# Block attention on Trainium2: two branches of one head group summed in one PSUM bank, the local one's probabilities scaled by GpSimd

## The reference, cut to what matters

```python
o_cmp = einsum(softmax(q @ kcmp - slope*dist), vcmp)          # p_c also picks the 8 blocks of o_sel
o_sel = einsum(softmax(q @ k_selected - slope*dist), v_selected)
o_win = einsum(softmax(q @ k_window - slope*dist), v_window)
gate  = sigmoid(gate_logits + gate_b)                         # three per head
o     = gate[..., 0:1]*o_cmp + gate[..., 1:2]*o_sel + gate[..., 2:3]*o_win
```

## Time and profile before

| | |
|---|---|
| runs | 4212.6, 4210.89, 4206.26 us; median 4210.89 |
| profiled execution | 4219.19 us |
| its span, first to last instruction | 4217.2 us |
| attention loop, first to last PE instruction | about 1591.7 to 2540.1 us |
| mean granted TensorE clock | 0.952 of 2.4 GHz |

### The profile page before, as it was taken

The page is one execution under the profiler, slowest core; times in us unless marked ns, Lnnn a source line. Parts: engine busy times, 40 slices in busy tenths (PEclk is TensorE's granted clock), DMA queues, the critical chain, the costliest instruction groups (busy, mean ns, idle before and its releaser), DMA issues. The chain is left out here.

```text
span 4217.2 us, 69303 instructions
## 1 busy us (share of the span) xinstructions
PE 3839.8 (91%) x26480; PEld 3139.9 (74%) x26481; DVE 2457.9 (58%) x4173; ACT 1996.7 (47%) x3165; POOL 578.8 (14%) x945
## 2 busy tenths in 40 slices
PE   7999999999988878999888877999599999999798
PEld 5777877777767646777777766999478888888687
DVE  2545555555556427777777655444576555567565
ACT  2434433344333216666666653222276555567565
POOL 1111111111121112112212210000110000001120
PEclk9999999999999978999999988999699999999899
DMA  4534434443333350000000006433388666689642
GB/s 129 152 99 111 134 107 111 123 118 92 106 98 88 78 123 23 14 13 19 16 19 19 21 13 190 133 124 105 150 332 325 235 237 228 226 318 363 252 149 94
DMA packets 512853, 557.18 MB, mean 132 GB/s; under 512 B 106188, under 2 KB 374476, under 8 KB 511532
## 3 DMA queue, kind: packets, MB, share of 16 engines
q1 hardware_dynamic: 479988, 461.10, 34.7%
q0 software_dynamic: 16416, 59.78, 3.8%
q10 hardware_dynamic: 16176, 32.55, 2.1%
HBM read 439.78 MB, written 113.57 MB: 131 GB/s over the span
## 5 line engine op out<-in xcount | busy, mean ns | idle before, releaser
L555 PE MATMUL fr_fb<-fr_hT_h,fr_w_h 128*128 128x512 f32 (+1 forms) x1312 | 536.1, 409 | 11.0 <-ACT fr_zs L836 7.6
L555 PE MATMUL fr_fb<-fr_hT_r,fr_w_h 128*128 128x512 f32 (+1 forms) x1312 | 531.9, 405 | 0.0
L555 PE MATMUL fr_fb<-fr_hT_h,fr_w_r 128*128 128x512 f32 (+1 forms) x1312 | 531.6, 405 | 0.0
L1005 DVE TENSOR_TENSOR fr_w_r<-fr_w_raw,fr_w_h 128x1024 fp32r<-128x1024 f32 (+1 forms) x164 | 197.9, 1207 | 498.4 <-ACT fr_w_h L809 497.4
L2065 DVE TENSOR_TENSOR aq_p_lo<-aq_t_bank,aq_p_hi 128x512 fp32r<-128x512 f32 x412 | 283.0, 689 | 192.1 <-ACT aq_p_hi L1958 184.8
L1958 ACT CAST aq_p_hi<-aq_t_bank 128x512 fp32r<-128x512 f32 x412 | 238.5, 581 | 249.7 <-PE aq_t_bank L1865 244.0
L836 ACT COPY fr_zs<-fr_fb 128x512 f32<-128x512 f32 (+1 forms) x148 | 87.0, 588 | 509.2 <-PE fr_fb L555 508.7
L555 PEld LDWEIGHTS fr_fb<-fr_hT_h,fr_w_h 128*128 128x128 f32 (+1 forms) x1312 | 248.8, 190 | 79.1 <-ACT fr_zs L836 13.2
L555 PEld LDWEIGHTS fr_fb<-fr_hT_h,fr_w_r 128*128 128x128 f32 (+1 forms) x1312 | 249.0, 190 | 63.4 <-issue 11.1
L555 PEld LDWEIGHTS fr_fb<-fr_hT_r,fr_w_h 128*128 128x128 f32 (+1 forms) x1312 | 249.1, 190 | 62.2 <-issue 10.9
L134 PE MATMUL ex_gu<-wx_gate_w,ex_xT 128*128 128x512 f32 x1176 | 288.5, 401 | 3.6 <-DVE ex_xT L2848 3.6
(11 more groups left out here) (495 smaller groups left out, 8672.0 us busy)
## 6 DMA issues: line engine op xcount, KB each, us to landing
wk_raw<-in_w_exp_gate_up SPq DMA_DIRECT2D x64, 2048.0 KB, 10.9
fr_w_raw<-in_w_in SPq DMA_DIRECT2D x160, 512.0 KB, 3.9
wk_raw<-in_w_exp_down SPq DMA_DIRECT2D x32, 2048.0 KB, 10.1
s_z<-fr_zs SPq DMA_DIRECT2D x160, 256.0 KB
s_rows<-ex_y ACTq DMA_DIRECT2D x50, 512.0 KB, 4.3
mx_mg<-s_z SPq DMA_DIRECT2D x32, 512.0 KB, 7.3
fr_zc<-s_z SPq DMA_DIRECT2D x15, 903.0 KB, 6.8
sh_shared<-in_x SPq DMA_DIRECT2D x16, 512.0 KB, 5.2
```

The source lines that it names most:

```text
L555: ins = pe.matmul(bank[0:cols_, :], (w_h, w_h, w_r)[p][:, k, c, 0:cols_].bitcast(F32R), (hT_h, hT_r, hT_h)[p][:, c, :].bitcast(F32R), star ...
L1005: dve.tensor_tensor(w_r[:, m % 2, :, 0:cols_].bitcast(F32R), w_raw[:, m % 2, :, 0:cols_], w_h[:, m % 2, :, 0:cols_], ALU.subtract).then_in ...
```

## The change

The units' order becomes selected, local, selected, local, both of the same pair. The pair's two units now share one sum in `o_bank`: the first `weigh` of the selected unit starts it and the last one of the local unit ends it. For that the local probabilities must carry the factor by which the local branch's weight differs from the selected one's. In the stage before, DVE turns gate 2 into gate 2 over gate 1, once. In the loop the new `ratios` (DVE, three small operations) makes that times the selected total over the local total, per head, and the new `scale` (POOL, four operations of up to 128x640) multiplies the local exponentials in place. A local unit's first `turn` waits for `scaled`. `ratios` and `scale` stand in step min(last run + 2, first turn - 1).

"back" comes once a pair, as four plain 128x128 transposes that fill `misc`; `combine` adds the halves by a reduction, multiplies by the weight and adds to y (three operations of 256 results each instead of four small ones or one). `take_out` comes once a pair, and waits for y instead of "back". "turn_y" moves behind the local unit of g = 1, that is two steps into the next selected unit. `select` always writes y by one DVE operation. "take_q" follows the last run of the local unit. `pair` goes. From t = 4 on the `small` places in `sc_even` and `sc_odd` begin with the selected unit.

```diff
         pairs = [(t, g) for t in reversed(range(NT)) for g in range(KV_HEADS)]
-        ahead = 2
-        self.units = [(t, g, WIN) for t, g in pairs[:ahead]]
-        for n, (t, g) in enumerate(pairs):
-            if n + ahead < len(pairs):
-                self.units.append((*pairs[n + ahead], WIN))
-            self.units.append((t, g, SEL))
+        self.units = [(t, g, b) for t, g in pairs for b in (SEL, WIN)]
         self.at = {unit: u for u, unit in enumerate(self.units)}
...
         f = self.first
-        self.small = self.at[WINDOW // P + 1, KV_HEADS - 1, SEL] + 1
+        self.small = self.at[WINDOW // P + 1, KV_HEADS - 1, WIN] + 1
         self.runs_at, self.run_end, self.begin, self.last = {}, [], [], []
...
             self.out_step[n] = later
-        self.out_step[0] = max(self.out_step[0], 6)
-        self.pe, self.act, self.dve, self.pool = {}, {}, {}, []
+        self.pe, self.act, self.dve, self.pool, self.ratios = {}, {}, {}, [], {}
         put = lambda table, step, *what: table.setdefault(step, []).append(what)
...
             if g == 0 and t + 2 < NT:
-                pool.append((self.last[self.at[t + 2, 1, SEL]] + 1, 2, n, "take_q", t, 0))
+                pool.append((self.last[self.at[t + 2, 1, WIN]] + 1, 2, n, "take_q", t, 0))
+            u = self.at[t, g, WIN]
+            step = min(self.last[u] + 2, f[u] - 1)
+            put(self.ratios, step, t, g)
+            pool.append((step, 1.5, n, "scale", t, g))
         self.lead = -min(m[0] for m in marks)
-        for u, (t, g, b) in enumerate(self.units):
-            marks.append((f[u + 1] + 2, 3, u, "back", t, 2 * g + b))
+        for n, (t, g) in enumerate(pairs):
+            marks.append((f[self.at[t, g, WIN] + 1] + 2, 3, n, "back", t, g))
         for t in range(NT):
-            marks.append((f[self.at[t, 1, SEL] + 1] + 3, 4, NT - t, "turn_y", t, 0))
+            marks.append((f[self.at[t, 1, WIN] + 1] + 3, 4, NT - t, "turn_y", t, 0))
         self.pool = [what[3:] for what in sorted(pool)]
...
             return ((0, 0), (1, 2 * (WINDOW + P)), (1, WINDOW + P), (1, 0))[(u - self.small) % 4]
-        return u % 2, RUN * (u // 2 % 2) if b == SEL and t < RUN // P else 0
+        return 1 if b == SEL else 0, RUN * (u // 2 % 2) if b == SEL and t < RUN // P else 0
...
     def reused(self, u):
-        return 5 <= u < len(self.units) and self.units[u][2] == self.units[u - 2][2] == SEL and self.units[u][0] >= RUN // P
+        return 2 <= u < len(self.units) and self.units[u][2] == SEL and self.units[u][0] >= RUN // P
...
         if u > self.at[RUN // P, KV_HEADS - 1, SEL]:
-            return (f[u - 1], (2 * f[u] + f[u - 1]) // 3) if u % 2 == 0 else (self.last[u - 1] + 1, f[u] - 2)
+            return (f[u - 1], (2 * f[u] + f[u - 1]) // 3) if self.units[u][2] == WIN else (self.last[u - 1] + 1, f[u] - 2)
         return f[u - 1], f[u] - 2
-
-    def out_is_first(self, t, g):
-        return self.misc["out", t, g] < self.misc["back", t, 2 * g + WIN]
...
-                step(pool.memset(pair[:, :], 0.0))
-                for d in range(2):
-                    masked(pair[:, :], [[-1, HD]], -d * HD, 1, 1.0, ALU.not_equal)
...
                 low(3)
+                by_branch = gates[:, :, :].rearrange("p t (h b) -> p b t h", b=3)
+                dve.wait_ge(g_done, 1)
+                dve.tensor_scalar(by_branch[:, 1, :, :], by_branch[:, 1, :, :], LEAST_GATE, None, ALU.max).then_inc(g_split, 1)
+                dve.wait_ge(g_split, 1)
+                dve.reciprocal(g_inv[:, :, :], by_branch[:, 1, :, :]).then_inc(g_split, 1)
+                dve.wait_ge(g_split, 2)
+                dve.tensor_tensor(by_branch[:, 2, :, :], by_branch[:, 2, :, :], g_inv[:, :, :], ALU.mult).then_inc(g_split, 1)
+                dve.wait_ge(g_split, 3)
                 dve.wait_ge(out_ok, 3)
...
                 def take_q(t):
-                    pool.wait_ge(s_made, F.run_end[F.at[t + 2, G - 1, SEL]])
+                    pool.wait_ge(s_made, F.run_end[F.at[t + 2, G - 1, WIN]])
                     split_q(pool, order(t))
...
                         pool.tensor_tensor(total_p, total_p, pct[0:N_CMP, h, :], ALU.add).then_inc(added, 1)
+
+                def scale(t, g):
+                    f, sc = front_no(t, g), sc_of(F.at[t, g, WIN])
+                    pool.wait_ge(ratio_ok, f + 1)
+                    for h in range(R):
+                        ins = pool.tensor_scalar(sc[:, h, :], sc[:, h, :], ratio[:, h:h + 1], None, ALU.mult)
+                    ins.then_inc(scaled, 1)
...
                     if kind == "back":
-                        pe.wait_ge(ot_ok, F.at[t, k // 2, k % 2] + 1)
+                        pe.wait_ge(ot_ok, front_no(t, k) + 1)
                         misc_free(n)
                         for h in range(R):
-                            ins = pe.matmul(misc[:, h * HD:(h + 1) * HD], oT[:, h, :], pair[:, :], start=True, stop=True)
+                            ins = pe.transpose(misc[:, h * P:(h + 1) * P], oT[:, h, :], ident[:, :])
                     if kind == "turn_y":
-                        pe.wait_ge(y_ok, F.at[t, G - 1, SEL] + 1)
+                        pe.wait_ge(y_ok, front_no(t, G - 1) + 1)
                         misc_free(n)
...
                     if n == F.first[u]:
-                        pe.wait_ge(exp_ok, R * (u + 1))
+                        t, g, b = F.units[u]
+                        if b == WIN:
+                            pe.wait_ge(scaled, front_no(t, g) + 1)
+                        else:
+                            pe.wait_ge(exp_ok, R * (u + 1))
                     if n >= 2:
...
                     t, g, b = F.units[u]
-                    first, last = n == F.first[u], n + 1 == F.first[u + 1]
+                    first, last = b == SEL and n == F.first[u], b == WIN and n + 1 == F.first[u + 1]
                     pe.wait_ge(lo_ok, n + 1)
                     if first and u:
-                        pe.wait_ge(ot_ok, u)
+                        pe.wait_ge(ot_ok, front_no(t, g))
                     for p in (p_hi, p_lo):
...
                         act.copy(flat(pct[0:N_CMP, :, :]), misc[0:N_CMP, :]).then_inc(misc_read, 1)
-                    if kind == "out" and F.out_is_first(t, k):
-                        act.wait_ge(misc_made, n + 1)
-                        act.wait_ge(imp_ok, f + 1)
-                        for h in range(R):
-                            c = 3 * (k * R + h)
-                            ins = act.activation(y[:, t % Y, k, h, :], misc[:, h * HD:(h + 1) * HD], ACT.Copy, scale=gates[:, t, c:c + 1])
-                        ins.then_inc(misc_read, 1)
                     if kind == "turn_y":
...
                 def take_out(n, u):
+                    t, g, b = F.units[u]
                     act.wait_ge(pv_made, n - 1)
-                    if u:
-                        t, g, b = F.units[u - 1]
-                        act.wait_ge(misc_made, F.misc["back", t, 2 * g + b] + 1)
+                    if u > 1:
+                        act.wait_ge(y_ok, front_no(t, g))
                     act.copy(flat(oT[:, :, :]), o_bank[:, :]).then_inc(ot_ok, 1)
...
                     ended = F.block[n - 2][0] if 0 <= n - 2 < F.n and n - 1 == F.first[F.block[n - 2][0] + 1] else None
+                    if ended is not None and F.units[ended][2] == SEL:
+                        ended = None
                     early = ended is not None and n > F.first[ended] + 2
...
                 v = Chain(dve, vec)
+                gate_of = lambda t, g, b: gates[:, t, 3 * R * g:3 * R * (g + 1)].rearrange("p (h b) -> p b h", b=3)[:, b, :]
+                wide_heads = lambda a: a.rearrange("p (h o) -> p h o", o=1).to_broadcast([P, R, HD])
...
-                def add_scaled(t, g, scale_of):
-                    for h in range(R):
-                        ins = dve.scalar_tensor_tensor(out=y[:, t % Y, g, h, :], in0=misc[:, h * HD:(h + 1) * HD], scalar=scale_of(h),
-                                                       in1=y[:, t % Y, g, h, :], op0=ALU.mult, op1=ALU.add)
-                    return ins
-
                 def select(n, t, g):
...
                     dve.wait_ge(misc_made, n + 1)
+                    if f:
+                        dve.wait_ge(sel_ok, f)
                     dve.tensor_tensor(imp[:, :], misc[:, R * HD:R * HD + N_SEL], keep_t[:, at], ALU.mult).then_inc(imp_ok, 1)
                     dve.wait_ge(imp_ok, f + 1)
-                    if not F.out_is_first(t, g):
-                        v.link(add_scaled(t, g, lambda h: gates[:, t, 3 * (g * R + h):3 * (g * R + h) + 1]))
-                        dve.sem_inc(misc_read, 1)
+                    v.link(dve.tensor_tensor(y[:, t % Y, g, :, :], misc[:, 0:R * HD].rearrange("p (h d) -> p h d", h=R),
+                                             wide_heads(gate_of(t, g, 0)), ALU.mult))
+                    dve.sem_inc(misc_read, 1)
                     v.link(dve.tensor_tensor(imp[:, :], imp[:, :], force_t[:, at], ALU.add))
...
```

(33 more changed lines are left out.)

16 lines of the change are left out of this document (10 added, 6 removed).

## The result

The change makes the kernel slower: 4325.4 us (4321.8 to 4328.6, four runs) against 4209.4 before on the same chip, a ratio of 1.0275 with a 95% interval of 1.0258 to 1.0293. That is +116 us where -19 was forecast (4192, range 4162 to 4230), outside the range.

A forecast was written before the change was run, and what follows sets the result against it. PE was taken to set the pace in selected stretches, chains of waits in local ones. Terms +22 - 46 + 4 + 8 - 3 + 3 - 7 = -19 us gave 4192 us, range 4162 to 4230.

The forecast's parts named there:

- (d): GpSimd's scaling: 0.75 us an operation, covered for t from 15 to 6, stalls at t = 5: +8 us, bounds 0 to 14.
- (f): End, pairs of t = 4 to 0: fewer "backs" -15, exposed scaling and ratios +12, shorter last chain -4: -7 us.
- (a): Loop start: first cast 26.5 us later, because selected unit 15,0 needs the whole front; net +22 us.
- (b): Local stretches: 2.1 us less in each of 22, from ACT's work and two waits: -46 us, bounds 20 to 86 saved.
- more comes back: Rival: local stretches fall to near PE's own work, 73 us saved instead of 46; total -46, 4165 us; chance 0.13.
- ScalarE holds: Rival: ScalarE holds the local stretches, only 19 us saved instead of 46; total +8, 4219 us; chance 0.15.
- (c): Selected stretches: DVE gains 1.3 us net, of which +0.2 a stretch comes through: +4 us, bounds -7 to +35.
- VectorE becomes the bound: Rival: in the selected stretches, via `p_lo`, 44 us instead of 4, from 95% DVE share; total +21, 4232; chance 0.15.
- (e): Joint at t = 4: eight runs fall into one step and PE waits for six masks: +3 us, bounds 0 to 6.
- Blocking of DVE and POOL: Rival: DVE's new small operations are held beside POOL's, 20 us in 32 pairs; total +1, 4212 us; chance 0.07.
- "wrong" ones: Signs against: selected stretches over 1 us longer with DVE over 95%; scalings over 1.2; local stretches 11 or more; `scaled` waits above t = 6.

The follow-up runs named there:

- scaling at 0.80 instead of 1.88 us: The changed kernel with each GpSimd scaling operation given a second step, a factor of 1: 4253.3 us, ratio 1.0100.
- the version with the scaling in two parts: The changed kernel, scaling the first key block of all heads as one broadcast product, then the rest head by head with two steps: 4239.5 us, ratio 1.0068.
- one-column run: The changed kernel with each GpSimd scaling operation cut to one column of its head, the other columns left unscaled: 4220.6 us, ratio 1.0028.
- experiment 6: Changed kernel with scaling in two parts (4239.5 us), then earlier local runs, later turn of y and rotated places (4205.7), old turn-back (4195.0), earlier normalisation (4188.8).

## Why the prediction was wrong

The step that failed is (d), GpSimd's scaling, with its price (0.75 us an operation, measured 1.88) and its cover (two plan steps "of some 2 us", measured 1.4 us for three). It was put at +8 us, and with the 12 of step (f) at 20. The error is 135 us (+116 against -19). Read against before, the chain of kernels splits it:

| | against before, us | step |
|---|---|---|
| changed kernel | +116 | |
| scaling at 0.80 instead of 1.88 us | +41 | price: 75 |
| no ratios, no scaling | -37 | ratios, and exposure at the assumed price: 78 |

Forecast for these: price as assumed, 0; exposure 8 of step (d) and 12 of step (f), together 20. That leaves 75 + 58 = 133 of the 135 us. In the traces, from first cast to last, the two steps are 89 and 64 us, since the profiled execution at 0.80 us was a short one; their sum is the same.

Without the 20, the forecast's own sum is -39, and the kernel without ratios and scaling measured -37. That near hit is luck: by its trace the local stretches of t = 15 to 5 took 212 us where the forecast has 224 with the joint, the selected ones 489 where it has 472, and the rest behind them 153 where it has 166. These errors of -12, +17 and -13 us largely cancel.

Step by step:

- **(a) the start** was right. From the loop's first PE instruction to the first cast it took 38.4 us against 11.7, so 26.7 more, forecast 26.5, bounds 22 to 31 (0.9 of it for gate operations ahead of this stretch, so 25.6 is what to compare). Its links held too: counted from the loop's start, the first mask table stood at 21.5 us where the forecast's working has 21.2, the last exponential ended at 37.1 against 36.1.
- **(b) the local stretches** came out right, 10.0 us where 12.16 - 2.1 = 10.06 was forecast, but partly by luck. The rivals "more comes back" and "ScalarE holds" (11.3 or more) are out for these stretches. Without the ratios they fall to 9.35 (196.3 over the same 21). The difference goes with the clock behind the stalls: PE is busy 176.3 us in them in the changed kernel and 151.4 without ratios. And the terms were others than forecast. PE's waits for the copy of `o_bank`, 18.6 us in the 19 stretches before, are gone and not halved, while its waits for `p_lo` grew from 6.6 us to 29.0 in 21.
- **(c) the selected stretches**: the mechanism was named and its size missed. Without ratios and scaling they grew by 21 us, not 4, and 16 of these go with the reduction. Its price was estimated rightly (0.69, measured 0.692). What failed is the share of it that comes through: 0.2 of 1.3 us was taken because DVE stood at 89% by the reckoning. One wait was put at nothing: the forecast moved the turn of y into these stretches as 0.35 us of PE's work, and PE waits there 16.4 us in eight for the combine to end (10.7 in eight before, in the local stretches). The rival "VectorE becomes the bound" had +44 us for these stretches, about twice too much, and a condition that the run doesn't show; DVE stood at 82%. DVE's added work itself, with the ratios, was 420.8 - 388.0 = 32.8 us, 1.5 a stretch, inside the 1.3 to 1.6 of the forecast.
- **(d) the scaling** failed twice. The price: a row of the same instruction, but with two steps, was taken for one with a single step, and the "upper end" of 1.26 was the row of another operation, no bound. And the cover: "at least two steps of some 2 us" was counted from the plan's step numbers. The ratios' operations come last in their step on DVE, 3.6 us behind its cast at 9,0, and PE's turn runs ahead of its own. Of three steps 1.4 us were left. The condition for the cover's end stood in the text (3.6 us a unit without it); at 0.80 us an operation ten units more paid than was thought, at 1.88 fourteen. What the forecast had nowhere is the clock behind a stall.
- **(e) the joint at t = 4**: +3 forecast with bounds 0 to 6, on a local stretch of 10.06, so 13.1 and at most 16.1. The stretch of 5,1 took 18.9 us in the changed kernel and 15.2 without ratios (12.6 before). It isn't the wait for masks that was forecast: PE waits 1.0 us for them in the changed kernel and is busy 17.9 us at a clock of 0.73, against 13.5 us at 1.00 without ratios.
- **(f) the end**: from selected unit 4,0 to the last cast it took 186.2 us against 183.9, so +2.3 where -3 was forecast up to there; without the ratios 152.8. The ratios and the scaling cost 33 us in the ten pairs and not 12: for the six units of t = 2 to 0 the operations were priced at 1 to 1.4 us a unit, and measured 2.4 (four times 0.60 at 128 columns) to 5.0. PE waited 24.9 us for GpSimd in these six. PE's waits for "take_q", 3.4 us in two before, are gone as forecast (-3). The -4 behind the last step was about 1: from the last cast to the attention's last instruction it took 12.4 us, before 13.5.
- **Blocking of DVE and POOL** is real and small. In the changed kernel, first DVE and then GpSimd at the same moment:

```profile
2416.52 2.21 DVE L2029 TENSOR_TENSOR aq_ratio<-aq_ratio,at_gates 128x4 f32<-128x4 f32 x1
```

```profile
2416.37 2.34 POOL L1493 TENSOR_TENSOR at_q_s<-at_q_raw,at_q_s 64x1024 fp32r<-64x1024 f32 x1
```

An operation of 0.165 us (median of 32) ended together with GpSimd's. But only four of the changed kernel's new two-input operations took over 0.6 us (2.21, 1.13, 0.90, 0.71), together 3.8 us more than their usual 0.16 and 0.42; the rival's 20 us were too much. The Trainium skill (SBUF — State Buffer, "Who interferes with whom") says that the second is fully blocked until the first ends; the trace agrees with the 2.21 us, and with the 1.13, which ended with another split of the queries. Beside the single-step scaling of 1.9 us the two longer ones were 0.28 and 0.48 us late, less than the rest of GpSimd's operation, which that rule would not give.

Of the signs named in the forecast, two of the "wrong" ones appeared at once: scalings over 1.2 us, and PE waiting for `scaled` at t above 6. The third, selected stretches over 1 us longer with DVE over 95%, appeared only by half.

What stays open: why the version with the scaling in two parts is 12 us slower than the one-column run though their seams are alike. Waits of 16 us for GpSimd's second part and for "normalise" could be named, but not how much of them is on the path, and the loop itself was only 6.5 us longer in the traces. No run holds the clock while a wait changes, so how much of a stall's price is the lower clock rests on the busy times of the same 4355 matmuls. And the parts in experiment 6 were tried together, so 12 to 16 us for the later turn of y rest on the waits and not on a run of its own.

## What to carry to other kernels

Price an operation by a row of the same form, down to whether it has one step or two; a row of another form is no bound. Cover for a moved operation is not a number of steps: take the time at which its engine reaches it, behind everything that is in program order ahead of it, and the time at which the waiting engine would otherwise start, and subtract. An engine at 80% of its time can still pass most of its added work on, where the bound engine waits for an operation right behind the new one: ask who waits for the end of the chain, not how full the engine is. And a stall of TensorE costs more than its length when the clock has fallen by its end.

## What the hardware showed unexpectedly

- GpSimd, on 128 partitions of fp32: `tensor_scalar` with one step took 0.60 us for 128 columns and 1.88 for 640, 2.5 ns a column; with a second step that changes nothing 0.37 and 0.80, 0.84 ns a column. A copy took 0.72 for 640.
- Even 128x1 took 0.28 us (median of 128) each, so four short ones cost 1.04 us.
- A broadcast product took 1.04 us for 512 columns and 4.45 for 2560: below the single-step form and above the two-step one.
- TensorE's clock: behind a wait of 6.10 us a turn took 1.11 us and not 0.60, at a granted clock of 0.50; behind one of 1.76 us at the same seam it took 0.66.
